# A two-part transformer, 256 tokens on one core: norms and the first two units of most stages by token tile, gates spread by a transfer

## What is computed

```python
h = rms_norm(x, pre[l]);            x = x + rms_norm(mixer(h), post_mix[l])        # first block
h = rms_norm(x, pre_ffn[l]);        x = x + rms_norm(ffn(h), post_ffn[l])
shift, scale, gate = ada(c)                                                        # second block
h = rmsnorm(x) * (1 + scale) + shift; x = x + gate * mixer(h)                      # and the same with ffn
ffn(h) = (silu(h @ w_gate) * (h @ w_up)) @ w_down
```

## Time and profile before

| what | us |
|---|---|
| median of 3 runs (lowest, highest) | 1897.62 (1897.14, 1897.76) |
| profiled execution: span from first to last instruction | 1895.6 |
| TensorE busy in it | 1866.6 (98%) |
| VectorE, ScalarE busy | 1355.3 (71%), 961.1 (51%) |

### The profile page before, as it was taken

The page is one execution under the profiler, slowest core; times in us unless marked ns, Lnnn a source line. Parts: engine busy times, 40 slices in busy tenths (PEclk is TensorE's granted clock), DMA queues, the critical chain, the costliest instruction groups (busy, mean ns, idle before and its releaser), DMA issues.

```text
span 1895.6 us, 34471 instructions
## 1 busy us (share of the span) xinstructions
PE 1866.6 (98%) x13496; PEld 1716.5 (91%) x13496; DVE 1355.3 (71%) x2194; ACT 961.1 (51%) x1486; POOL 69.5 (4%) x82
## 2 busy tenths in 40 slices
PE   8999999999999999999999999999999999999998
PEld 8989999998999987999989799999989999989997
DVE  6758888775878877888877587886555556766555
ACT  7755334766533466533473553346554334764333
POOL 3003000000000000000000000003300000000000
PEclk9999999999999999999999999999999999999999
DMA  8538987533788742688844378875335554325552
GB/s 307 186 126 260 352 306 304 189 134 134 291 326 308 297 168 95 243 336 308 315 182 140 112 289 328 308 282 221 114 126 202 193 180 154 131 92 198 190 187 89
DMA packets 60653, 412.39 MB, mean 218 GB/s; under 512 B 8624, under 2 KB 8816, under 8 KB 11904
## 3 DMA queue, kind: packets, MB, share of 16 engines
q1 hardware_dynamic: 56016, 401.33, 57.6%
q0 software_dynamic: 4528, 9.56, 1.9%
HBM read 409.71 MB, written 3.16 MB: 218 GB/s over the span
## 4 chain that ended last, share of the span: by engine, by line
PE 89%; DVE 5%; ACT 3%; issue 1%; DVEq 1%; ACTq 1%; DMA 0%; SPq 0%
PE psu L509 35%; PE psy L677 19%; PE psy L571 7%; PE psy L563 5%; PE psy L617 5%; PE psu L526 4%; PE psm L753 3%; PE psy L550 2%; PE psu L738 2%; PE pso L724 1%; PE psy L640 1%; DVE wlo L881 1%; DVE x L1167 1%; PE psy L1684 1%; ACT work L797 1%
## 5 line engine op out<-in xcount | busy, mean ns | idle before, releaser
L872 ACT CAST whi<-raw 128x2048 fp32r<-128x2048 f32 (+1 forms) x281 | 536.3, 1909 | 599.1 <-PE psu L509 400.5
L881 DVE TENSOR_TENSOR wlo<-raw,whi 128x2048 fp32r<-128x2048 f32 (+5 forms) x306 | 646.6, 2115 | 254.9 <-ACT whi L872 254.5
L509 PE MATMUL psu<-hlo,whi 128*128 128x256 f32 x1920 | 536.6, 280 | 0.0
L509 PE MATMUL psu<-hhi,whi 128*128 128x256 f32 x1920 | 536.6, 279 | 0.0
L509 PE MATMUL psu<-hhi,wlo 128*128 128x256 f32 x1920 | 536.6, 279 | 0.0
L509 PEld LDWEIGHTS psu<-hhi,whi 128*128 128x128 f32 x1920 | 361.4, 188 | 2.3
L509 PEld LDWEIGHTS psu<-hlo,whi 128*128 128x128 f32 x1920 | 361.3, 188 | 2.3
L509 PEld LDWEIGHTS psu<-hhi,wlo 128*128 128x128 f32 x1920 | 361.4, 188 | 0.0
L1083 DVE CUSTOM_DVE_ANT_0 ada_raw<-ada_raw,cvec 128x1024 f32<-128x1024 f32 x192 | 227.1, 1220 | 1.9 <-DMA ada_raw<-ada 1.9
L677 PE MATMUL psy<-whi,ahi 128*128 128x512 f32 x528 | 210.3, 398 | 0.0
L677 PE MATMUL psy<-wlo,ahi 128*128 128x512 f32 x528 | 208.2, 394 | 0.0
(11 more groups left out here) (341 smaller groups left out, 3013.4 us busy)
## 6 DMA issues: line engine op xcount, KB each, us to landing
raw<-wts SPq DMA_DIRECT2D x280, 1024.0 KB, 4.9
ada_raw<-ada SPq DMA_DIRECT2D x96, 1024.0 KB, 4.9
dense_bias<-rel_bias POOLq DMA_DIRECT2D x32, 64.0 KB, 9.7
nab<-dense_bias SPq DMA_DIRECT2D x2, 1024.0 KB, 7.6
ada_raw<-fox_rows POOLq DMA_DIRECT2D x4, 512.0 KB, 12.5
cb<-cst POOLq DMA_DIRECT2D x1, 1408.0 KB, 9.7
cb<-cst SPq DMA_DIRECT2D x1, 1056.0 KB, 10.1
x<-x_in SPq DMA_DIRECT2D x2, 512.0 KB, 4.5
```

What stands on the lines that cost most here:

```text
L509: last = mm(psu[:, bank, cc * SEQ:(cc + 1) * SEQ], a[:, cols], h[:, kt, :], start=(kt == 0 and j == 0), stop=(kt == KT - 1 and j == 2))
L872: nc.scalar.copy(whi[:, part_of(c), 0:n], raw[:, slot_of(c), 0:n]).then_inc(hi_done, 1)
L881: last = nc.vector.tensor_tensor(wlo[:, part_of(c), cols], raw[:, slot_of(c), cols], whi[:, part_of(c), cols].bitcast(f32), ALU.subtract)
```

## The change

1. The norm goes by token tile. `pe_norm(pe, m, t)` transposes one tile into banks chosen by `turned`; `act_norm1`, `act_norm2`, `dve_split1`, `dve_split2` work on 128 tokens. `act_stage` and `dve_stage` write out the order of the whole boundary: the first tile's root and pairs before the second tile's sums, update and root.
2. The first two units are made with tokens on partitions (`pe_token_lead`): steps of two k for both units, first tile first; the second tile's transposes stand before step 3 (in the opening before step 1). GLA and FOX keep the lead in columns, with the second tile's transposes right behind the first's. Since the feed-forward's first two units then come out with tokens on partitions, four transposes (`act_columns`) turn the two activations, ScalarE copies them to `ahi` and VectorE makes `alo`, both after unit 2.
3. The cast of the second unit of a stage is made in two halves (`act_lead_hi`), and the first half of its subtraction (`dve_lead_lo`) stands ahead of the update of x.
4. `pe_gate` and `act_gate` go. GpSimd writes each gate row to DRAM and loads it into `gain` for all partitions (`load_gate`); the host orders the gate columns for it. Fillers: 4, 6, 4, 6 at the four stages of the first block, none in the second (before: 4, 14, 12, 14, and 6 at the second block's start).

```diff
+TOKEN_LEAD = "00 01 02 10 11 12 03 13"
+TOKEN_STEPS = [[(u, i // 4, range(i % 4 * 2, i % 4 * 2 + 2)) for u in range(2)] for i in range(6)] + [
+    [(u, 1, range(4, KT))] for u in range(2)]
...
+MIX = Plan([2 if u is None else 4 for u in W_IN1], [3, 4, 1] + [2] * 11 + [1] * 20 + [2] * 4, range(12, 32),
+           [24, 25, 28, 29, 30, 31, 33, 35], TOKEN_LEAD,
...
+SWA = Plan([4] * 6, [2, 2, 3, 1] + [2] * 4 + [1] * 15 + [2, 2, 1, 2, 2], range(6, 22), [11, 13, 15, 17, 20, 21, 23, 25],
+           TOKEN_LEAD, [2, 4, 6, 8, 13, 17, 20, 24], 16)
...
+
+        def turned(m, t, k):
+            first = (psy[:, 0], psy[:, 1]) if m % 2 else (psu[:, 0], psu[:, 1])
+            bank = ((pso[:], psm[:], *first) if t == 0 else (psy[:, 2], psy[:, 3], pso[:], psm[:]))[k // 2]
+            return bank[:, k % 2 * P:(k % 2 + 1) * P]
...
+            def load_gate(i):
+
+                n, which = i // 2, i % 2
+                pool.wait_ge(ada_done, STEPS * (n + 1))
+                pool.dma_start(gate_rows[i].rearrange("(p j) -> p j", p=P),
+                               mod[:, n, 16 + 24 * which:24 + 24 * which]).then_inc(gate_stored, 16)
+                pool.wait_ge(gate_stored, 16 * (i + 1))
+                pool.wait_ge(x_ready, 4 * (2 * DEPTH1 + i + 1))
+                pool.dma_start(gain[:], gate_rows[i].partition_broadcast(P)).then_inc(gain_loaded, 16)
...
             pool.dma_start(cb[:, 0:NCB2], cst2).then_inc(cb2_loaded, 16)
+            load_gate(0)
             pool.wait_ge(o_evac, item0[0] + 16)
...
+            for i in range(1, 5):
+                load_gate(i)
             pool.wait_ge(fox_c, 1)
...
-            pool.dma_start(nab[:, 0:D], final_gain[0].partition_broadcast(P)).then_inc(gain_loaded, 16)
+            for i in range(5, 2 * DEPTH2):
+                load_gate(i)
...
+        def pe_token_lead(pe, l, c, i, q, outs, widths=(2 * P, 2 * P)):
+            opening = (l, c) == (0, 0)
+            for u, t, kts in (OPENING_STEPS if opening else TOKEN_STEPS)[i]:
+                k, width = part_of(c + u), widths[u]
+                toks = slice(t * P, t * P + P)
+                for kt in kts:
+                    if t == 0 and kt % 4 == 0:
+                        if opening and u == 0 and kt == 0:
+                            pe.wait_ge(opening_lo, 1)
+                        elif not opening and u == 1 and kt == 0:
+                            pe.wait_ge(lead_lo, q)
+                        elif opening or u == kt // 4:
+                            pe.wait_ge(lo_done, unit_no(l, c + u) + 1)
+                    if u == 0:
+                        pe.wait_ge(h_ready if t else h0_ready, 8 * q + kt + 1)
+                    for p, (h, a) in enumerate(((hhi, whi[:, k]), (hlo, whi[:, k]), (hhi, wlo[:, k]))):
+                        last = mm(outs[u][:, t * width:(t + 1) * width], h[:, kt, toks], a[:, kt * width:(kt + 1) * width],
+                                  start=(t == 0 and kt == 0 and p == 0), stop=(kt == KT - 1 and p == 2), skip_group_check=True)
+                if t == 1 and kts[-1] == KT - 1:
                     last.then_inc(unit_mm, 1)
...
+        def pe_norm(pe, m, t, idle=0):
+            pe.wait_ge(xn_ready, NT * m + t + 1)
             for kt in range(KT):
+                if (t, kt) == (1, 4):
+                    pe.wait_ge(h0_ready, 8 * m + 4)
+                mm(turned(m, t, kt), x[:, t, kt * P:(kt + 1) * P], rows[:, t, 0:P], start=True, stop=True).then_inc(tr_done, 1)
...
+            def act_columns():
+                for f, bank in ((0, par), (1, 1 - par)):
+                    pe.wait_ge(bank_free, bo + f + 1)
+                    for t in range(NT):
+                        last = nc.tensor.transpose(psy[:, f, t * P:(t + 1) * P], a32[:, bank, t * P:(t + 1) * P], ident[:])
+                    last.then_inc(a_tr, 1)
...
-            pe_lead_cols(pe, l, c0, (par, 1 - par), 2 * n + 1)
+            for i in range(8):
+                if i == 3:
+                    pe_norm(pe, 2 * n + 1, 1)
+                pe_token_lead(pe, l, c0, i, 2 * n + 1, (psu[:, par], psu[:, 1 - par]))
...
                     gu(c, i, 2 + 4 * i + 2 * k, par)
+                    if opens and k == 0:
+                        act_columns()
                     gu(c + 1, i, 3 + 4 * i + 2 * k, 1 - par)
...
+        def act_lead_hi(act, l, c, i=0):
+            if last_unit(l, c + TURN * i):
+                return
+            u = unit_no(l, c, i)
+            act.wait_ge(raw_loaded[slot_of(c)], (l * (PER1 // RAW) + i * (TURN // RAW) + c // RAW + 1) * 16)
+            act.wait_ge(unit_mm, u - SPLIT + 1)
+            n = size_of(l, c + TURN * i)
+            for at, signal in ((0, lead_hi), (n // 2, hi_done)):
+                nc.scalar.copy(whi[:, part_of(c), at:at + n // 2], raw[:, slot_of(c), at:at + n // 2]).then_inc(signal, 1)
+        def dve_lead_lo(dve, l, c, m):
+            n = size_of(l, c)
+            dve.wait_ge(lead_hi, m)
+            nc.vector.tensor_tensor(wlo[:, part_of(c), 0:n // 2], raw[:, slot_of(c), 0:n // 2],
+                                    whi[:, part_of(c), 0:n // 2].bitcast(f32), ALU.subtract).then_inc(lead_lo, 1)
...
+        def act_norm2(act, q, n, which, t, ks):
+
+            toks, ks_ = slice(t * P, t * P + P), slice(ks[0], ks[-1] + 1)
+            if (t, ks) == (0, (4, 5)):
+                act.wait_ge(hw_done, q - 2 * DEPTH1 + 1)
+            else:
+                act.wait_ge(tr_done, 16 * q + 8 * t + ks[-1] + 1)
                 for k in ks:
+                    nc.scalar.activation(hw[:, k, toks], turned(q, t, k), ACT.Identity, scale=acol[:, 8 * which + k:8 * which + k + 1],
+                                         bias=mod[:, n, 24 * which + k:24 * which + k + 1])
                 nc.scalar.drain()
+            nc.scalar.copy(hhi[:, ks_, toks], hw[:, ks_, toks]).then_inc(hhi_done, 2)
...
+        def act_stage(act, m, end):
+            u = m - 1
+            def norm(t, ks):
+                if m < 2 * DEPTH1:
+                    act_norm1(act, m, pcol[:, m // 2, 8 * (m % 2):8 * (m % 2) + 8], t, ks)
+                else:
+                    act_norm2(act, m, m // 2 - DEPTH1, m % 2, t, ks)
+
+            if u < 2 * DEPTH1:
+                for b in range(3):
+                    act_post(act, u, b, *end)
+                act_square(act, m, 0, 0)
+                act_square(act, m, 0, 1)
+                act_post(act, u, 3, *end)
+            else:
+                act_square(act, m, 0, 0)
+                act_square(act, m, 0, 1)
+                act_square(act, m, 1, 0)
+            if m < 2 * DEPTH1:
+                act.wait_ge(pcol_loaded, 16 * (m // 2 + 1))
+            else:
+                act.wait_ge(acol_ready, m - 2 * DEPTH1 + 1)
+            norm(0, (0, 1))
+            norm(0, (2, 3))
+            if u < 2 * DEPTH1:
+                act_square(act, m, 1, 0)
+                norm(0, (4, 5))
+                act_square(act, m, 1, 1)
+            else:
+                act_square(act, m, 1, 1)
+                norm(0, (4, 5))
+            norm(0, (6, 7))
+            for ks in PAIRS:
+                norm(1, ks)
...
+        def dve_stage(dve, m, end, lead):
+            u = m - 1
+            dve_lead_lo(dve, *lead, m)
+            dve.wait_ge(gain_loaded, 16 * m)
+            if u < 2 * DEPTH1:
+                dve_gained(dve, u, 0)
+                dve_gained(dve, u, 1)
+                dve_update(dve, u, 0, 0)
+                dve_update(dve, u, 0, 1)
+                dve_gained(dve, u, 2)
+                dve_scale(dve, m, 0)
+                dve_gained(dve, u, 3)
+                dve_update(dve, u, 1, 0)
+            else:
+                for t, half in ((0, 0), (0, 1), (1, 0)):
+                    dve_gated(dve, u, t, half, end)
+                dve_scale(dve, m, 0)
+                dve_gated(dve, u, 1, 1, end)
+            if m < 2 * DEPTH1:
+                dve.wait_ge(pcol_loaded, 16 * (m // 2 + 1))
+                split = lambda t, ks: dve_split1(dve, m, pcol[:, m // 2, 8 * (m % 2):8 * (m % 2) + 8], t, ks)
+            else:
+                split = lambda t, ks: dve_split2(dve, m, t, ks)
+            split(0, (0, 1))
+            if u < 2 * DEPTH1:
+                dve_update(dve, u, 1, 1)
+            dve_lo(dve, *lead, quarters=(2, 4))
+            split(0, (2, 3))
+            if m >= 2 * DEPTH1:
+                dve_columns2(dve, m, m // 2 - DEPTH1, m % 2, (4, 5))
+            dve_scale(dve, m, 1)
+            split(0, (4, 5))
+            split(0, (6, 7))
+            for ks in PAIRS:
+                split(1, ks)
...
                 act.wait_ge(unit_mm, unit_no(l, c0 + f) + 1)
-                nc.scalar.activation(sg[:, bank], psu[:, bank, 0:SEQ], ACT.Silu).then_inc(silu_done, 1)
+                nc.scalar.activation(fold(sg[:, bank], NT, P), fold(psu[:, bank], NT, 2 * P)[:, :, 0:P], ACT.Silu).then_inc(silu_done, 1)
                 act_hi(act, l, c0 + f + SPLIT)
+            for f in range(2):
+                act.wait_ge(a_tr, 2 * n + f + 1)
```

(29 more changed lines are left out.)

379 lines of the change are left out of this document (140 added, 239 removed).

## The result

The changed kernel takes **1921.88 us** (median of 4 runs, 1919.73 to 1923.03), the kernel before beside it 1897.69: ratio **1.0125, 95% interval 1.0113 to 1.0138**, 24.2 us slower. The prediction said 1911.5 with a range of 1899 to 1926. Sign and range held; of the size it had only 57%, and the measured time lies 0.9 us above the forecast's own narrower range (1904 to 1921).

The account below looks back on a forecast made before the run. The kernel was taken as bound by TensorE's stream of products, losing time only in waits. 7.2 + 4.9 + 0.6 - 0.5 + 0.2 + 1.5 = +13.9 us on 1895.6, plus 2.0 for the median, gave 1911.5, range 1899 to 1926.

Parts of the forecast that it names:

- Price of a piece: ScalarE's norm operation on 128 columns: 0.45 us, against 557 ns on 256 columns; a pair with its cast 1.17 us.
- The rival of the short pieces: ScalarE's 128-column pieces cost about half of 256-column ones, so boundaries come out even: 1896 to 1901; chance 0.20.
- Feed-forward boundary: Second block's feed-forward starts: first product sooner, at +4.4, but unit 2 late; four boundaries cost +7.2 us.
- ScalarE makes its four pairs to +14.25: Second block's feed-forward starts: ScalarE's second-tile pairs run from +9.55 to +14.25, where the norm ends at +11.66 today.
- GLA and FOX: Starts of these two stages: first product at +9.5 instead of +6.26, unit 2 later; +2.45 us each, +4.9.
- the late second scaled identity: GLA and FOX starts: VectorE makes the second tile's scaled identity only by +6.7, so its transposes end at +8.7.
- SWA starts: Starts of the second block's two SWA stages: +0.2 us for the first, about 0 for the second.
- Opening: Kernel start: a wait of 1.0 us and the second transposes put unit 2 at 25.6 instead of 24.17, +1.5 us.
- First block: Starts after a mixer in the first block: sooner first product, offset by new transposes and waits; +0.3 each, +0.6 us.
- Gates: Gate transfers have a whole stage as cover and cost 0; removing the gate products is worth 0.
- Clock, rival B: TensorE's idle at second-block starts halves its clock, some 2.2 us each: 1916 at GLA and FOX alone, 1929 at all eight; chance 0.13.
- D: First product not sooner than E+6 because VectorE's moved subtraction delays the quarters: another +1.5 at nine boundaries, 1925; chance 0.05.

Follow-up runs that it names:

- e3_cast: Changed kernel with ScalarE's cast of unit 2 moved ahead of the second tile's pairs in the second block's feed-forward and SWA stages: 1914.56 us.
- e8_root: Changed kernel with the second tile's root and scaled identity moved earlier at GLA and FOX, pieces still 128 tokens: 1927.65 us.
- e4_wide: Changed kernel with GLA and FOX started as before: early second root, 256-token norm pieces, half of the column pieces on VectorE: 1914.12 us.
- e1_order: Changed kernel with the opening lead reordered, all eight pieces of unit 0 before those of unit 1: 1915.83 us.
- e10_turns: e6_all with each of the four transposes of the first two activations made twice in all six feed-forwards: 1903.53 us.
- e5_gate: Kernel before with only the gates changed to GpSimd transfers, gate products and copies removed, no fillers in their place: 1897.10 us, ratio 0.9998.
- e7_share: Changed kernel with VectorE making the values of the second tile's first and third pairs in all eight second-block starts, casts staying on ScalarE: 1927.17 us.
- e6_all: Changed kernel with opening reordered, zero products in second-block waits, unit 2's cast moved earlier, GLA and FOX started as before: 1901.62 us, ratio 1.0021.

## Why the prediction was right in sign and short in size

- **Price of a piece**: 0.45 us taken, 0.452 measured. A pair 1.17, measured 1.18 (1437.90 to 1439.08). The rival of the short pieces fell with it.
- **Feed-forward boundary**: first product +4.4, measured +4.5 where VectorE was free and +4.8 to +5.05 behind GLA and the SWA stages (the 0.2 and 0.5 us for late VectorE were taken right); end of the lead +17.8, measured +18.0 to +19.1; unit 2 +18.85, measured +19.5 to +20.3, with the wait on VectorE's product that was named. The mechanism was right (e3_cast); the terms, 7.2 us with their 1.2, measured 9.4. The step mis-sized is "ScalarE makes its four pairs to +14.25": the last cast ended at +14.9, and everything behind it moved along. Another 1.3 us is the clock in two of the four.
- **GLA and FOX**: 4.9 taken, 5.75 measured, 0.8 of it FOX's low stretch. First product +9.5, measured +9.8 (GLA) and +10.5 (FOX, with its low stretch). But the cause that I named, the late second scaled identity, was wrong (e8_root). The 128-token pieces on ScalarE in tile order decide (e4_wide), their size and their number together.
- **SWA starts**: the step that failed is "+0.2" and "about 0". I walked these starts only to the end of their leads and never asked for unit 2, though the queue I had just walked in the feed-forwards (pairs, cast of unit 2, subtraction) is the same. They lost 1.9 and 1.0; e3_cast gave back 1.8 and 1.3, for the first with a low stretch in both profiles.
- **Opening**: the step that failed is "11.45 + 1.0 + 1.95 + 11.2 = 25.6, +1.5 us". The head was right (first product 11.44, unit 2 at 25.18, +1.0). It stopped there. The new order of the pieces ends unit 0 at 24.06, 3.7 us later than before, while unit 1 ends 1.0 later, and the end of unit 0 releases a cast, a raw slot and a table: 4.8 us more, all cured by the order (e1_order).
- **First block**: +0.3 each, measured +0.2; mixer 1 -0.5, measured -0.9. The activation transposes: 0.44, measured 0.36 from their start to the next product and 0.44 for a second set (e10_turns).
- **Gates** 0: right (e5_gate).
- **Clock, rival B**: between my cases. Drops came in four of eight starts, at 0.5 to 0.8 us each, 2.6 us in the profiled execution; my estimate of 2.2 us for each was three times too dear at these starts, where the stretch falls in part on waits. In the opening, where the profiled execution had none, other kernels paid 1.5 us for one. The Trainium skill's warning (TensorE: Matmul & The Clock Gate, Why this matters for your kernels) held in its direction; but of the two longest waits, 3.16 us at GLA and 3.17 at FOX, only the second was followed by a drop, and waits of 1.86 and 2.13 us were too.
- **D**: out. VectorE's moved subtraction never kept a first feed-forward product of the second block behind E+5.1.

Sum of the misses against +23.4 in the trace: opening 4.1, SWA starts 2.7, feed-forwards of the second block 2.2, GLA and FOX 0.85, first block -0.5; together 9.3 of the 9.5 us between +13.9 and +23.4. That the measured time fell inside the stated range owes something to luck: the opening's 4.1 us and the SWA stages' 2.7 stood in no rival, and the range had room for them only because it took in the lower part of the clock rival's.

No version made here beats the kernel before. What the stages show as gains of the change (0.9 us at mixer 1, 0.25 at the second SWA) is 0.06% together, below what a measurement of this kernel can tell, so a kernel with only these was not run. The four repairs are worth knowing all the same: with its queues in order and GLA and FOX left as they were, the change costs 0.2% (0.12 to 0.31), and as it stands 1.25%.

## What to carry to other kernels

When a lead is reordered, walk not only when it begins and ends but when *each unit* ends, and then follow what that end releases through every queue (cast, subtraction, raw slot, the next transfer behind it). When an in-order queue gets smaller and more pieces, look for the one long item behind them that could go into a wait ahead of them: here one cast moved up gave back 7 us. And work that is moved to an idle engine in the middle of a chain can come back as a wait, when that engine's queue starts it only behind the other engine's last result (e7_share).

## What the runs showed that I had not expected

- Waits of 1.9 to 3.2 us in a stream that is otherwise dense came with a granted clock of 0.5 for 3.41 us (6.83 in four places, in e7_share and e8_root) in some starts and not in others with the same waits: at four of the eight starts in the changed kernel, at six of them and in the opening in e3_cast, nowhere inside a stage in e6_all. One cost 0.5 to 0.8 us at the starts of the changed kernel and its like, nothing that shows in e5_gate, and 0.1 or 1.5 us in the opening, by what came behind it. The kernels with such waits also spread more from run to run (3.3 us, against 0.9 for the kernel before).
- The same 1056 KB table, to the same place, landed after 10.1, 14.6 and 9.0 us depending on when it was issued (25.50, 29.20, 25.26).
